# A hybrid attention and convolution layer: attention steps three to a dense unit, key loads moved ahead, attention rows reloaded in pairs

## The chip, the cores and the metric

The kernel runs on one core of one Trainium2 chip. The metric is the device time of one execution in microseconds. A run with the hardware profiler gives the trace that the rows below come from.

## The reference

One layer for 512 latent and 128 context tokens of width 2048, in float32: a modulated norm; one input projection into a gated convolution branch, grouped queries, keys, values and two branch gates; the two branches; a gated sum, an output projection, and a routed expert network. Cut to what the change touches:

```python
h = rmsnorm(x, n1g) * (1 + sc1) + sh1
glu_in, q, k, v, ga, gb = jnp.split(h @ w_in, SPLITS, axis=-1)
conv_out = conformer_conv(glu_in, ...)
# per head, 16 heads in 4 key groups of 4 query heads; blocks of 128 queries;
# latent blocks read keys of a window of +-128 tokens and all 256 cached context keys,
# the context block reads the 128 context keys
m = jnp.maximum(jnp.max(sc, axis=-1, keepdims=True), sk)
p = jnp.exp(sc - m)
den = jnp.sum(p, axis=-1, keepdims=True) + jnp.exp(sk - m)
att = einsum(p / den, vals)
attn_out = att @ w_attn_out
mixed = (sigmoid(ga) * conv_out + sigmoid(gb) * attn_out) @ w_out
```

The modulation vectors (adaLN) come from `silu(cond) @ w_ada`, 96 blocks of 128 columns.

## The kernel before, in words

Every matrix product in float32 is made of three products of split operands: the weights of a unit (128 output columns, 2048 x 128) are loaded into `raw`, a ring of four slots; ScalarE casts them into `whi` (L846), VectorE subtracts to get `wlo` (L1185), and TensorE runs 96 matmuls (L579 to L581), six for each of the sixteen k-steps, against `hhi` and `hlo`, the split activations. The split of a unit is made two units ahead. An adaLN block is 1 MB of weights too, goes through the same ring, and is used unsplit (L563), closed by a small transpose (L566) that frees its slot; ScalarE reads its result out (L859, L853).

The program of each engine is written out by hand; engines wait for each other by semaphores, each engine working in its own order. The stage of interest makes the 32 units of the branch gates (tanh, L1007, stored to `gates_tanh`, L455). It is a loop over the four key groups, eight units to a pass. Beside the dense work of the pass run:

- the 20 attention steps of the group (4 heads x 5 query blocks, `STEPS`; the fifth block of each head, j = 4, is the short context one). A step on TensorE: scores (L653 to L656), a part of the unit's dense k-steps, transposes of the normalised probabilities (L666), an adaLN block if it is the unit's first or second step, and the product with the values (L678). On VectorE: maxima (L1304, L1308, L1315), then sums and normalisation (L1324 to L1329). On ScalarE: exponentials (L960 to L968), the copy of the transposed probabilities (L975, L977), the copy of the head's output (L984), which POOL's queue stores into `att` (L451);
- 16 adaLN blocks, two to a unit;
- 62 taps of the depthwise convolution on VectorE (L1344, L1348).

`CUT` deals the steps to units: before, 2 and 3 alternately, so the eighth unit of a group has three. The weights' splits for later units (`next_unit`) stand, on ScalarE and VectorE, behind the first step's softmax of the following unit, except that of the eighth unit, which stands at the end of the pass, ahead of the next pass's first step. In the order of the ring the loads of a unit are its own weights, then the two adaLN blocks; each waits until the load four places earlier has been used up.

POOL's queue loads a group's keys (`ktg`), values (`vg`) and first queries (`qh`) at the top of the pass, behind all stores of the pass before. Behind the last group it waits for the stores of outputs and gates, then reloads the attention rows, one 128 x 640 block to a load, into a ring of four (`att4`, L469); ScalarE casts each into `hhi` (L1028), VectorE subtracts into `hlo` (L1381), and the first unit of the attention projection takes each k-step as it comes.

```python
cuts = [KT * x // len(steps) for x in range(len(steps) + 1)]
for x, n in enumerate(steps):
    qk(i, n)
    dense(d, d, k % 2, k % 2, hhi, hlo, cuts[x], cuts[x + 1], 0, KT)
    turn(i, n)
    if x < 2:
        ada_unit(...)
    pv(i, n)
```

Of the kernel before, what the change touches and what calls it, by code (L numbers as in the profile page):

```python
# [41 lines left out]
US = 8  # L42
# [26 lines left out]
def build(nc, a, out):  # L69
# [62 lines left out]
    zt, o = at("zt", [128, CT, ZW], F32, Y0)  # L132
    ctmp, o = at("ctmp", [128, CO], F32, o)
    ktg, o = at("ktg", [128, N + PAST], F32, o)
    vg, o = at("vg", [128, (N + PAST) // 128, HD], F32, o)
# [24 lines left out]
    gl, o = at("gl", [128, 2, N], F32, o)  # L160
    att4, _ = at("att4", [128, 4, N], F32, o - 2 * N * 4)
    mo, o = at("mo", [128, 2, N], F32, o)
# [90 lines left out]
    vec_done = sem("vec_done")  # L253
    act_done = sem("act_done")
    gsc_ready = sem("gsc_ready")
# [50 lines left out]
    NS = len(STEPS)  # L306
    CUT = [NS * k // US for k in range(US + 1)]

# [65 lines left out]
    def pool_program(pool):  # L374
# [65 lines left out]

        with pool.Fori(0, NKV) as i:
            load_group(i)
            load_q(i, 1)
            for k in range(US):
                for n in range(CUT[k], CUT[k + 1]):
                    h, j = STEPS[n]
                    if j == 0 and 0 < h and h + 1 < GROUP:
                        load_q(i, h + 1)
                    pool.wait_ge(att_out, i * NS + (n + 1) + 1)
                    settle()  # L450
                    pool.dma_start(at_d[i * GROUP + h][:, 128 * j:128 * j + 128],  # L451
                                   ao[:, n % 2, :]).then_inc(att_stored[n % 2], 16)
                pool.wait_ge(th_ready, i * US + (k + 1))
                settle()
                pool.dma_start(th_d[i * US + k], th[:, k % 2, :]).then_inc(th_stored[k % 2], 16)  # L455


        for b in range(2):
            pool.wait_ge(att_stored[b], 16 * (NKV * NS // 2))
            pool.wait_ge(th_stored[b], 16 * (SN // 2))  # L460

# [3 lines left out]

        for m in range(KT):
            if m >= 4:
                pool.wait_ge(attn_lo, m - 3)
            pool.dma_start(att4[:, m % 4, :], at_d[m]).then_inc(attn_loaded[m % 4], 16)  # L469
        pool.wait_ge(attn_lo, KT)  # L470
# [83 lines left out]
    def tensor_program(pe):  # L554
# [127 lines left out]
        with pe.Fori(0, SN // US) as i:  # L682
            for k in range(US):
                d = i * US + (QN + GN + k)
                dense_start(d, QN + GN + k, i, US)
                steps = list(range(CUT[k], CUT[k + 1]))
                cuts = [KT * x // len(steps) for x in range(len(steps) + 1)]
                for x, n in enumerate(steps):
                    qk(i, n)
                    dense(d, d, k % 2, k % 2, hhi, hlo, cuts[x], cuts[x + 1], 0, KT)  # L690
                    turn(i, n)
                    if x < 2:
                        at_ = G_S + 3 * k + 1 + x
                        ada_unit(at_ % RAW, at_ // RAW + i * (3 * US // RAW),
                                 i * (2 * US) + (RAW + A1 + 2 * k + x), pt[:, 1, :], row1[0:2, :])
                    pv(i, n)
        pe.wait_ge(ada_read, RAW + ADA)
# [143 lines left out]
    def scalar_program(act):  # L841
# [144 lines left out]
        def stage_s(i):  # L986
# [5 lines left out]
            for k in range(US):  # L992
                steps = list(range(CUT[k], CUT[k + 1]))
                for x, n in enumerate(steps):
                    softmax(i, n)
                    if x == 0 and k:
                        next_unit(k - 1)
                    turned(i, n)
                    if x < 2:
                        at_ = G_S + 3 * k + 1 + x  # L1000
                        ada_read_out(at_ % RAW, at_ // RAW + i * (3 * US // RAW), i * (2 * US) + (A1 + 2 * k + x - 1),
                                     pt[:, 1, :], row1[0:2, :])
                    head_out(i, n)
                act.wait_ge(dense_mm, i * US + (QN + GN + k + 1 + CREDIT))
# [21 lines left out]
        for m in range(KT):  # L1026
            act.wait_ge(attn_loaded[m % 4], 16 * (m // 4 + 1))
            nc.scalar.copy(hhi[:, m, :], att4[:, m % 4, :]).then_inc(attn_hi, 1)  # L1028

# [143 lines left out]
    def vector_program(vec):  # L1173
# [180 lines left out]
        def stage_s(i):  # L1354
            def next_unit(k):
                slot, use, d2 = ahead(i, k, US, G_S, 3, QN + GN, SN, G_T)
                split_lo(slot, use, d2, k % 2)

            for k in range(US):
                steps = list(range(CUT[k], CUT[k + 1]))  # L1360
                for x, n in enumerate(steps):
                    maxima(i, n)
                    normalise(i, n)
                    if x == 0 and k:
                        next_unit(k - 1)
                    conv(i, k, x, len(steps))
            next_unit(US - 1)
# [11 lines left out]
        for m in range(KT):  # L1379
            vec.wait_ge(attn_hi, m + 1)  # L1380
            nc.vector.tensor_tensor(hlo[:, m, :], att4[:, m % 4, :], hhi[:, m, :].bitcast(F32),  # L1381
                                    ALU.subtract).then_inc(attn_lo, 1)
# [440 lines left out]
```

## Time and profile before

| | |
|---|---|
| median of 3 runs | 3484.56 us (3480.05 to 3485.72) |
| the profiled execution | 3483.9 us |
| its span, first to last instruction | 3482.3 us, mean granted clock 0.975 |
| TensorE busy | 3293.6 us, 95% |
| VectorE busy | 1938.5 us, 56% |
| ScalarE busy | 1391.7 us, 40% |
| DMA | 746 MB, mean 214 GB/s |

The span is shorter than the profiled execution's own time by what lies around it. The stage with the attention steps stands from about 744 to 1661 us of the span, the first unit of the attention projection behind it to 1696. Busy time of TensorE is of pipelined matmuls whose ends are modelled; the granted clock is given as a share of full speed.

### The profile page before, as it was taken

The page shows a single profiled execution, that of the slowest core. Times are in us where ns is not written, and L with a number is a line of the kernel's source. Part 1 is how long each engine was busy: PE and PEld are TensorE (multiplying, and loading weights), DVE is VectorE, ACT ScalarE, POOL GpSimd, SP SyncE. Part 2 cuts the span into 40 slices and gives each one's busy share as a digit, 9 for nine tenths or more (in the row PEclk, how much of TensorE's full clock was granted, in tenths as well). Part 3 has the DMA queues.
Part 4 walks back from the last instruction along what each step waited for, and adds up shares of the span by engine and source line. Part 5 has one row for each costly group of instructions (what it writes and reads, how often), then busy time and mean ns, then how long its engine had stood idle before and what let it go on. Part 6 is the DMA issues. An engine that isn't in the chain of part 4 may idle for free.

```text
span 3482.3 us, 52715 instructions
## 1 busy us (share of the span) xinstructions
PE 3293.6 (95%) x20485; PEld 2765.2 (79%) x20485; DVE 1938.5 (56%) x1987; ACT 1391.7 (40%) x1669; POOL 280.5 (8%) x445
## 2 busy tenths in 40 slices
PE   7699999999989899899899999959999999999995
PEld 5499999998888888788799999946666666666663
DVE  3223332135444445454642533369998999899994
ACT  2311111122323232223331212137777777777774
POOL 0001110000010000000100111110000000000000
PEclk9899999999999999999999999979999999999997
DMA  7533332223333333333433454379999999999994
GB/s 295 202 109 127 124 117 99 81 81 139 134 136 143 133 143 131 134 141 130 168 119 118 179 163 136 99 259 364 400 376 374 391 390 371 381 391 386 374 386 146
DMA packets 124020, 745.97 MB, mean 214 GB/s; under 512 B 16720, under 2 KB 27024, under 8 KB 44096
## 3 DMA queue, kind: packets, MB, share of 16 engines
q1 hardware_dynamic: 96368, 631.28, 47.5%
q0 software_dynamic: 27504, 112.60, 10.5%
q8 instruction: 107, 1.75, 0.2%
q14 instruction: 41, 0.34, 0.0%
HBM read 681.60 MB, written 55.66 MB: 212 GB/s over the span
## 4 chain that ended last, share of the span: by engine, by line
PE 79%; DVE 7%; issue 5%; ACT 2%; DMA 2%; POOLq 0%; SPq 0%; POOL 0%; ACTq 0%; DVEq 0%
PE pu L813 20%; PE pu L579 15%; PE pu L580 15%; PE pu L581 15%; PE pt L563 7%; DVE elo L1603 4%; PE pt L678 2%; ACT ehi L1108 2%; PE ps L653 1%; DVE xe L1615 1%; PE pt L666 1%; PE ps L654 1%; DMA tokens_acc<-ysl,idx_all 1%; PE ps L784 1%; DMA att<-att 1%
## 5 line engine op out<-in xcount | busy, mean ns | idle before, releaser
L579 PE MATMUL pu<-hhi,whi 128*128 128x320 f32 x3328 | 1050.3, 316 | 50.1 <-DVE wlo L1185 32.1
L580 PE MATMUL pu<-hlo,whi 128*128 128x320 f32 x3328 | 1033.4, 311 | 0.0
L581 PE MATMUL pu<-hhi,wlo 128*128 128x320 f32 x3328 | 1033.2, 310 | 0.0
L1603 DVE TENSOR_TENSOR elo<-ering,ehi 128x2048 fp32r<-128x2048 f32 x384 | 874.7, 2288 | 107.0 <-ACT ehi L1108 103.8
L1108 ACT CAST ehi<-ering 128x2048 fp32r<-128x2048 f32 x384 | 731.3, 1912 | 238.3 <-PE pu L813 238.2
L579 PEld LDWEIGHTS pu<-hhi,whi 128*128 128x128 f32 x3328 | 629.9, 189 | 54.1 <-issue 43.1
L580 PEld LDWEIGHTS pu<-hlo,whi 128*128 128x128 f32 x3328 | 629.9, 189 | 2.0
L581 PEld LDWEIGHTS pu<-hhi,wlo 128*128 128x128 f32 x3328 | 629.4, 189 | 0.0
L846 ACT CAST whi<-raw 128x2048 fp32r<-128x2048 f32 x112 | 213.0, 1902 | 481.7 <-PE pu L581 463.5
L1185 DVE TENSOR_TENSOR wlo<-raw,whi 128x2048 fp32r<-128x2048 f32 x112 | 256.6, 2291 | 255.4 <-ACT whi L846 255.0
L813 PE MATMUL pu<-ehi,xhi 128*80 128x512 f32 x1024 | 322.0, 395 | 2.2
L813 PE MATMUL pu<-ehi,xlo 128*80 128x512 f32 x1024 | 320.3, 394 | 0.0
L813 PE MATMUL pu<-elo,xhi 128*80 128x512 f32 x1024 | 320.0, 393 | 0.0
L563 PE MATMUL pt<-raw,cond 128*2 128x128 f32 x2048 | 233.9, 273 | 0.0
L1348 DVE SCALAR_TENSOR_TENSOR ctmp<-zt,taps,ctmp 128x670 f32<-128x670 f32 x232 | 212.5, 916 | 29.2 <-DVE ctmp L1348 19.8
L813 PEld LDWEIGHTS pu<-ehi,xhi 128*80 128x80 f32 x1024 | 149.4, 148 | 89.8 <-DVE elo L1603 9.3
L813 PEld LDWEIGHTS pu<-elo,xhi 128*80 128x80 f32 x1024 | 151.6, 148 | 85.5 <-issue 0.7
L813 PEld LDWEIGHTS pu<-ehi,xlo 128*80 128x80 f32 x1024 | 151.5, 148 | 85.6 <-issue 0.7
L563 PEld LDWEIGHTS pt<-raw,cond 128*2 128x2 f32 x2048 | 168.7, 85 | 57.2 <-issue 10.7
L813 PE MATMUL pu<-ehi,hthi 128*80 128x512 f32 x512 | 162.9, 399 | 0.0
L813 PE MATMUL pu<-elo,hthi 128*80 128x512 f32 x512 | 159.8, 393 | 0.0
L813 PE MATMUL pu<-ehi,htlo 128*80 128x512 f32 x512 | 159.7, 393 | 0.0
(264 smaller groups left out, 2854.9 us busy)
## 6 DMA issues: line engine op xcount, KB each, us to landing
ering<-in_w_experts SPq DMA_DIRECT2D x384, 1024.0 KB, 8.2
raw<-in_w_ada SPq DMA_DIRECT2D x96, 1024.0 KB, 5.0
raw<-in_w_in SPq DMA_DIRECT2D x72, 1024.0 KB, 4.9
raw<-in_w_attn_out SPq DMA_DIRECT2D x16, 1024.0 KB, 5.2
raw<-in_w_out SPq DMA_DIRECT2D x16, 1024.0 KB, 4.9
gates_tanh<-th POOLq DMA_DIRECT2D x32, 320.0 KB, 3.2
gl<-gates_tanh POOLq DMA_DIRECT2D x32, 320.0 KB, 3.4
raw<-in_w_conv_out SPq DMA_DIRECT2D x8, 1024.0 KB, 4.8
```

The costliest lines, as they stand in the source:

```text
L563: last = nc.tensor.matmul(bank[0:2, 0:128], cond[:, kt, :], raw[:, slot, kt * 128:kt * 128 + 128], start=kt == 0, stop=kt == KT - 1)
L579: nc.tensor.matmul(o, whi[:, dk, w:w + 128], hi[:, kt, cols], start=kt == 0, stop=False)
L580: nc.tensor.matmul(o, whi[:, dk, w:w + 128], lo[:, kt, cols], start=False, stop=False)
L581: last = nc.tensor.matmul(o, wlo[:, dk, w:w + 128], hi[:, kt, cols], start=False, stop=kt == kts - 1)
L653: nc.tensor.matmul(ps[:, 0, 0:128 * (hi - lo)], qb, ktg[:, 128 * lo:128 * hi], start=True, stop=True)
L678: last = nc.tensor.matmul(pt[:, 0, 0:128], vg[:, v, :], pt_sb[:, 128 * b:128 * b + 128], start=b == 0, stop=b == len(vs) - 1)
L813: last = nc.tensor.matmul(pu[0:SLOTS, 2 * (h % 2) + c, :], left, ring[:, j % AHEAD, w:w + 512], start=k == 0 and left is hi and ring is eh ...
L846: nc.scalar.copy(whi[:, dk, :], raw[:, slot, :]).then_inc(hi_ready, 1)
L1108: nc.scalar.copy(ehi[:, j % AHEAD, :], ering[:, slot, :]).then_inc(ex_hi, 1)
L1185: nc.vector.tensor_tensor(wlo[:, dk, :], raw[:, slot, :], whi[:, dk, :].bitcast(F32), ALU.subtract).then_inc(lo_ready, 1)
L1348: nc.vector.scalar_tensor_tensor(out=dst, in0=ztf[:, ds(zb, CO)], scalar=w, in1=ctmp[:, :], op0=ALU.mult, op1=ALU.add).then_inc(conv_done, 1)
L1603: nc.vector.tensor_tensor(elo[:, j % AHEAD, :], ering[:, slot, :], ehi[:, j % AHEAD, :].bitcast(F32), ALU.subtract).then_inc(ex_lo, 1)
```

## The change

`CUT` becomes three steps to a unit: units one to six of a group have three steps, the seventh two, the eighth none. The eighth unit's dense work is still made in two parts, each with its adaLN block behind it; VectorE makes all its taps in one piece. The loads of the next group's keys, values and queries move from the top of the pass to before the store of the eighth unit's gates; the loop on POOL's queue runs over three groups, the first group's loads stand ahead of it and the last group behind it. The attention rows come back in pairs, eight loads of 640 KB, into a ring of eight blocks (`att8`) that lies over the keys, values and attention buffers; the wait for the gates' stores moves behind these loads. An unused semaphore goes.

```diff
@@ memory
+    att8, _ = at("att8", [128, 8, N], F32, o)
     ktg, o = at("ktg", [128, N + PAST], F32, o)
...
-    att4, _ = at("att4", [128, 4, N], F32, o - 2 * N * 4)
@@ steps of a unit
-    CUT = [NS * k // US for k in range(US + 1)]
+    CUT = [min(3 * k, NS) for k in range(US + 1)]
@@ POOL's queue
-        with pool.Fori(0, NKV) as i:
-            load_group(i)
-            load_q(i, 1)
+        def stage_s(i, following):
             for k in range(US):
                 for n in range(CUT[k], CUT[k + 1]):
...
+                if k == US - 1 and following is not None:
+                    load_group(following)
+                    load_q(following, 1)
                 pool.wait_ge(th_ready, i * US + (k + 1))
...
+        load_group(0)
+        load_q(0, 1)
+        with pool.Fori(0, NKV - 1) as i:
+            stage_s(i, i + 1)
+        stage_s(NKV - 1, None)
 
         for b in range(2):
             pool.wait_ge(att_stored[b], 16 * (NKV * NS // 2))
-            pool.wait_ge(th_stored[b], 16 * (SN // 2))
...
-        for m in range(KT):
+        for m in range(KT // 2):
             if m >= 4:
-                pool.wait_ge(attn_lo, m - 3)
-            pool.dma_start(att4[:, m % 4, :], at_d[m]).then_inc(attn_loaded[m % 4], 16)
+                pool.wait_ge(attn_lo, 2 * (m - 3))
+            pool.dma_start(att8[:, 2 * (m % 4):2 * (m % 4) + 2, :],
+                           at_d[2 * m:2 * m + 2].rearrange("h p n -> p h n")).then_inc(attn_loaded[m % 4], 16)
+        for b in range(2):
+            pool.wait_ge(th_stored[b], 16 * (SN // 2))
@@ TensorE, the units
                 steps = list(range(CUT[k], CUT[k + 1]))
-                cuts = [KT * x // len(steps) for x in range(len(steps) + 1)]
-                for x, n in enumerate(steps):
-                    qk(i, n)
-                    dense(d, d, k % 2, k % 2, hhi, hlo, cuts[x], cuts[x + 1], 0, KT)
-                    turn(i, n)
+                parts = max(2, len(steps))
+                for x in range(parts):
+                    n = steps[x] if steps else None
+                    if steps:
+                        qk(i, n)
+                    dense(d, d, k % 2, k % 2, hhi, hlo, KT * x // parts, KT * (x + 1) // parts, 0, KT)
+                    if steps:
+                        turn(i, n)
                     if x < 2:
...
-                    pv(i, n)
+                    if steps:
+                        pv(i, n)
@@ ScalarE, the same; then the attention rows
-            act.wait_ge(attn_loaded[m % 4], 16 * (m // 4 + 1))
-            nc.scalar.copy(hhi[:, m, :], att4[:, m % 4, :]).then_inc(attn_hi, 1)
+            act.wait_ge(attn_loaded[m // 2 % 4], 16 * (m // 8 + 1))
+            nc.scalar.copy(hhi[:, m, :], att8[:, m % 8, :]).then_inc(attn_hi, 1)
@@ VectorE, the units
-                for x, n in enumerate(steps):
-                    maxima(i, n)
-                    normalise(i, n)
+                parts = max(1, len(steps))
+                for x in range(parts):
+                    if steps:
+                        maxima(i, steps[x])
+                        normalise(i, steps[x])
                     if x == 0 and k:
                         next_unit(k - 1)
-                    conv(i, k, x, len(steps))
+                    conv(i, k, x, parts)
```

TensorE at the end of a group's pass. The second adaLN block of the eighth unit (`raw`, `cond`, 16 matmuls, waits for its slot's load) and what follows it stood so before:

```order
L563 MATMUL pt<-raw,cond 2x128 [waits ada_read]
L563 MATMUL pt<-raw,cond 2x128 x15
L566 MATMUL pt<-ident,row_73 128x2
L676 REGISTER_ALU
L678 MATMUL pt<-pt_sb,vg 128x128 [waits att_pt]
L678 MATMUL pt<-pt_sb,vg 128x128 x3
L656 MATMUL ps<-ktg,qh 128x128 [waits att_pt,att_exp]
```

and stands so now (the branch leads to the scores of the next group's first step):

```order
L569 REGISTER_ALU [waits raw_loaded3]
L571 MATMUL pt<-raw,cond 2x128 [waits ada_read]
L571 MATMUL pt<-raw,cond 2x128 x15
L574 MATMUL pt<-ident,row_73 128x2
L690 REGISTER_ALU
L690 COMPARE_AND_BRANCH
```

Before, a whole step with a third of the unit's dense work followed the block; now the pass ends with it.

ScalarE at the same place, from the second adaLN read-out to the pass's end and the next pass's first exponential. Before:

```order
L859 COPY row_73<-pt 2x128 [waits raw_freed3]
L853 ISA
L853 ACTIVATE mod<-pt,bada 128x2
L983 ISA [waits att_pv]
L984 COPY ao<-pt 128x128 [waits att_stored0]
L966 ACTIVATE pexp,dn<-ps,nm 128x128 [waits att_nm]
...
L1007 ACTIVATE th<-pu 128x640 [waits th_stored1,dense_mm]
L1010 REGISTER_ALU
L846 CAST whi<-raw 128x2048 [waits th_ready,dense_mm,raw_loaded3]
L1014 ISA [waits hi_ready]
```

Now:

```order
L871 COPY row_73<-pt 2x128 [waits raw_freed3]
L865 ISA
L865 ACTIVATE mod<-pt,bada 128x2
L1020 REGISTER_ALU
L1023 ACTIVATE th<-pu 128x640 [waits th_stored1,dense_mm]
L1026 REGISTER_ALU
L858 CAST whi<-raw 128x2048 [waits th_ready,dense_mm,raw_loaded3]
L1030 ISA [waits hi_ready]
L1031 ISA [waits att_stored0]
L1033 REGISTER_ALU [waits th_stored1,att_stored1,th_stored0]
L1033 COMPARE_AND_BRANCH
L972 ACTIVATE pexp,dn<-sm,nm 128x256 [waits att_nm]
```

The cast of weights from slot 3, the slot that the second adaLN block frees (`raw_freed3`), was parted from that block by a whole step and is now parted from it by the read-out and the tanh.

## Rows read from the trace of the kernel before

**Rows 1.** The page, part 1: busy time, share of the span, instructions of each engine.
```profile
PE 3293.6 (95%) x20485; PEld 2765.2 (79%) x20485; DVE 1938.5 (56%) x1987; ACT 1391.7 (40%) x1669; POOL 280.5 (8%) x445
```
**Rows 2.** Waits of TensorE: waiting group, releaser: us in total, times, longest.
```profile
PE ps L653 <- DMA ktg<-in_cache_k: 25.9, 3, 8.9
...
PE pu L579 <- DVE hlo L1381: 14.3, 6, 9.8
...
PE pt L678 <- ACT pt_sb L975: 5.7, 16, 0.4
...
PE pt L666 <- DVE pn L1329: 0.6, 1, 0.6
```
**Rows 3.** The chain in order of time, first group's end: start us, us, what.
```profile
965.98 0.27 ACT ao L984
...
970.46 3.75 DMA ktg<-in_cache_k
```
**Rows 4.** Stretches: us, busy (count) of PE, PEld, DVE, ACT, POOL, PEclk, DMA share, GB/s.
```profile
974.50:979.40 4.90, 4.85 (x16) 4.53 (x17) 1.13 (x4) 1.24 (x5) 0.00 (x0) 0.50 0.21 82
1700.00:1710.00 10.00, 10.00 (x70) 10.00 (x69) 9.86 (x2) 0.00 (x0) 0.00 (x0) 1.00 0.41 139
```
**Rows 5.** Timeline, first group's end: start us, us, engine, line, op [idle before <-releaser].
```profile
958.18 0.22 PE L566 MATMUL pt<-ident,row 2*128 2x2 f32 x1
...
958.44 0.26 ACT L859 COPY row<-pt 2x128 f32<-2x128 f32 x1 [3.15 <-PE pt L566]
...
958.58 0.33 SPq L321 DMA_DIRECT2D raw<-in_w_in  x1
...
967.01 1.90 ACT L846 CAST whi<-raw 128x2048 fp32r<-128x2048 f32 x1 [0.17 <-ACT th L1007]
```
**Rows 6.** Weight load L321, from issue: the one of 958.6, then of 1168.5.
```profile
DMA to landing us min/median/max: 4.9/4.9/4.9
...
DMA to landing us min/median/max: 7.3/7.3/7.3
```
**Rows 7.** Timeline where the stage begins.
```profile
744.42 0.59 PE L653 MATMUL ps<-ktg,qh 128*128 128x256 f32 x2
...
744.68 1.90 ACT L846 CAST whi<-raw 128x2048 fp32r<-128x2048 f32 x1 [11.36 <-PE pu L581]
...
753.12 0.66 PE L666 MATMUL pt<-ident,pn 128*128 128x128 f32 x4 [0.64 <-DVE pn L1329]
```
**Rows 8.** Timeline: a step with five key blocks, and a short third step.
```profile
877.31 0.27 PE L666 MATMUL ps<-ident,pn 128*128 128x128 f32 x1
...
877.62 0.58 ACT L975 COPY pt_sb<-pt 128x512 f32<-128x512 f32 x1 [4.72 <-PE ps L666]
878.10 0.27 ACT L977 COPY pt_sb<-ps 128x128 f32<-128x128 f32 x1
...
1660.99 0.49 PE L678 MATMUL pt<-pt_sb,vg 128*128 128x128 f32 x2 [0.35 <-ACT pt_sb L975]
```
**Rows 9.** Timeline, first unit of the attention projection.
```profile
1671.45 0.60 PE L579 MATMUL pu<-hhi,whi 128*128 128x320 f32 x1 [9.82 <-DVE hlo L1381]
...
1696.26 1.90 ACT L846 CAST whi<-raw 128x2048 fp32r<-128x2048 f32 x1 [3.76 <-PE pu L581]
```
**Rows 10.** The chain in order of time, behind the last group.
```profile
1663.28 2.44 DMA gates_tanh<-th
...
1666.87 6.12 DMA att<-att
...
1673.01 0.73 ACT hhi L1028
...
1673.77 0.83 DVE hlo L1381
```
**Rows 11.** DMA issues: KB, median us to landing; then L321 at 1654 to 1655.
```profile
att<-att POOLq DMA_DIRECT2D x16, 320.0 KB, 3.6
...
DMA to landing us min/median/max: 5.1/6.4/7.8
```

More of the change, by code:

```diff
@@ L253, in build @@
     vec_done = sem("vec_done")
-    act_done = sem("act_done")
     gsc_ready = sem("gsc_ready")
@@ L993, in stage_s @@
                 steps = list(range(CUT[k], CUT[k + 1]))
-                for x, n in enumerate(steps):
-                    softmax(i, n)
+                for x in range(max(2, len(steps))):
+                    n = steps[x] if steps else None
+                    if steps:
+                        softmax(i, n)
                     if x == 0 and k:
                         next_unit(k - 1)
-                    turned(i, n)
+                    if steps:
+                        turned(i, n)
                     if x < 2:
@@ L1002, in stage_s @@
                                      pt[:, 1, :], row1[0:2, :])
-                    head_out(i, n)
+                    if steps:
+                        head_out(i, n)
                 act.wait_ge(dense_mm, i * US + (QN + GN + k + 1 + CREDIT))
@@ L1360, in stage_s @@
                 steps = list(range(CUT[k], CUT[k + 1]))
-                for x, n in enumerate(steps):
-                    maxima(i, n)
-                    normalise(i, n)
+                parts = max(1, len(steps))
+                for x in range(parts):
+                    if steps:
+                        maxima(i, steps[x])
+                        normalise(i, steps[x])
                     if x == 0 and k:
                         next_unit(k - 1)
-                    conv(i, k, x, len(steps))
+                    conv(i, k, x, parts)
             next_unit(US - 1)
@@ L1380, in vector_program @@
             vec.wait_ge(attn_hi, m + 1)
-            nc.vector.tensor_tensor(hlo[:, m, :], att4[:, m % 4, :], hhi[:, m, :].bitcast(F32),
+            nc.vector.tensor_tensor(hlo[:, m, :], att8[:, m % 8, :], hhi[:, m, :].bitcast(F32),
                                     ALU.subtract).then_inc(attn_lo, 1)
```

## The prediction

> **What bounds the kernel now.** I read the page's totals first: TensorE is busy 95% of the span [rows 1], so what TensorE does, or is kept from doing, is the time, and work of the other engines costs nothing unless TensorE ends up waiting for it. Next, TensorE's own waits, longest first: in the stage that the change touches (about 744 to 1696 us) two entries matter, 25.9 us in three waits of the score matmuls L653 for the keys, and 14.3 us in six waits for the split attention rows (`hlo`, L1381), the longest 9.8 us [rows 2]. The chain around the first group's end says why the keys are late: ScalarE copies the last head's output at 965.98, and only behind that, and behind two stores and a query load on the POOL queue, is the key load issued; it ends at 974.21 [rows 3]. The stretches add a second price: behind the idle time come 4.9 us at a granted clock of 0.50 (the 1.2 GHz level), against 1.00 later [rows 4]. So each group's end costs about 8.6 us of idle and 2.4 us of half speed, 11 us, three times over.
>
> All sums below are against the profiled execution, 3483.9 us; the median of the runs shown is 0.7 us higher, 3484.6.
>
> **1. Key wait removed.** The next group's loads are now issued before the store of the eighth unit, when the last attention step is one whole unit past. Cover: that unit, at least 13.7 us of dense work (96 matmuls at 70 in 10.00 us [rows 4]). Gain 25.9 us of idle, and 3 x 2.4 = 7.3 us of half speed.
>
> **2. What is late next.** ScalarE and VectorE split the weights of a group's tenth dense unit (the next group's second) at the end of the group's code, ahead of the first softmax and the first maxima of the next group. Those weights go into the ring slot that the eighth unit's second adaLN block frees. Before, that slot was freed with a whole attention step still to come: TensorE's closing transpose of the adaLN block starts at 958.18, SP issues the load at 958.58, and the cast starts at 967.01 right behind the tanh, with no wait for the load [rows 5]. After, the eighth unit is two halves of dense work with an adaLN block behind each, so this block is the last thing in the unit. Call the start of its transpose f. The load is issued at f+0.4 and lands 4.9 us later [rows 6], at f+5.3; ScalarE casts, VectorE subtracts, and only then come maxima, exponential and normalisation of step 0. The same sequence stands once in the trace, where the stage begins: from the start of the cast at 744.68 to the transposes at 753.12 it takes 8.44 us [rows 7]. So the first transposes of the new group can run at f+13.75.
>
> TensorE is there earlier. At the stage's beginning the scores start at 744.42 and TensorE, with eight of the sixteen k-steps under the step, is at the transposes 0.64 us before they may run [rows 7]: 8.06 us. Now a first part holds five k-steps: 18 matmuls fewer, at 70 in 10.00 us [rows 4] 2.6 us less, so 5.5 us. Scores start about 0.2 after f: ready at f+5.7. Wait 13.75 - 5.7 = 8.05, three times 24.2 us. An idle stretch like the old one should again bring the lower clock; I take the same 7.3 us. **Group ends: -25.9 - 7.3 + 24.2 + 7.3 = -1.7 us.** The load is the unknown: the same kind of load one unit earlier took 7.3 us [rows 6], which adds 2.4 per group end; the clock may cost 0 or, as after the wait at 1671, some 3.9 us each.
>
> **3. Third steps without cover.** A unit has two adaLN blocks. Behind the transposes of a step's first and second part such a block runs while ScalarE copies the probabilities; a third step has none, and TensorE waits for the copy. Before, the four third steps of a group were all the short context step (one transpose, wait 0.35 us, 5.7 in 16) [rows 2, 8]. After, the steps stand three to a unit, so the third ones are steps 2, 5, 8, 11, 14 and 17: three with five key blocks, two with four, one short. With five blocks the last transpose ends at 877.31 + 0.27 = 877.58, the first copy runs from 877.62 for 0.58 and the second ends at 878.37; with 0.05 us from copy to matmul (my estimate of the signalling) the wait is 0.84. With four blocks there is the first copy alone: 0.04 + 0.58 + 0.05 = 0.67 [rows 8]. Per group 3 x 0.84 + 2 x 0.67 + 0.35 - 4 x 0.35 = 2.8 us, **four groups +11.2 us**. Ends: 0 if something fills the wait (I see nothing in TensorE's order that could), 11.2 as worked.
>
> **4. First step of the stage.** Its transposes may not run before 753.12 whatever TensorE does, and it arrives 2.6 us earlier: **+2.6 us**.
>
> **5. Steps with five k-steps over them** (the other long first and second parts): the wait for the normalised rows L1329 occurred once among 80 steps [rows 2], and the thirds that are now long have six k-steps. Hidden, 0.
>
> **6. Behind the last group.** Before: the last unit ends at about 1661.4, its gates' store has to land (2.44 us in the chain) before the first attention load is issued, half a microsecond ahead of 1666.87, and TensorE restarts at 1671.45; the first unit of the projection lasts until ScalarE's cast of 1696.26 can start [rows 9, 10]. That is 24.8 us for 96 matmuls which, at 70 in 10.00 us, need 13.7: the ring of four lets a load go only when a row is split, and one such load took 6.12 us in the chain [rows 10]. After: the store is no longer waited for, -2.4, but tanh stands behind the adaLN read-out, two small copies of which one is 0.26 [rows 5], so about 0.5, so the first load goes out about 3.0 after the unit's end. It is 640 KB now. Bounds: a single 320 KB row block took 3.6 median; 1 MB loads issued together took 5.1 and 7.8 [rows 11]. I take 5.2, since two weight loads are in flight beside it, then cast 0.73, subtraction 0.83 [rows 10] and 0.2 of signalling: restart 10.0 after the unit's end, as before. Then all four pairs are under way and the fifth is issued after two rows are split, about 8 k-steps ahead of need, so TensorE runs through: 13.7 plus 3.2 for a half-speed stretch (between 2.4 and 3.9) = 16.9. **Gain 7.9 us.** Ends: 2 if the pairs land as late as 7.8, 11 if there is no half speed at all.
>
> By the Trainium skill (DMA: Bandwidth & Descriptors, Anatomy of one DMA — SWDGE (gpsimd) path) such a transfer takes 2.0 us and bytes over 436 GB/s, so 3.5 us for a pair; the sum would be 1.7 us lower by it. The trace's 3.6 us median for half the bytes speaks against relying on it here.
>
> **Sum**: -1.7 + 11.2 + 2.6 - 7.9 = +4.2; 3483.9 + 4.2 = 3488.1, and 3489 beside the median. A measurement here can tell about 0.2% from no change, 7 us: from 3477.6 to 3491.5 is the same. So: no difference that can be measured, leaning to slower.
>
> **Rivals.**
> - *The group ends are simply freed.* Needs the tenth unit's weights to be in place when tanh ends. For: they were, before [rows 5]. Against: the slot is freed by the unit's last act. Time: 3489 - 24.2 - 7.3 = 3457. Chance 0.12.
> - *The weight load at the group end lands late* (slower). Place: the load issued at f+0.4, with an adaLN block's load right behind it and the gates' store beside it. Price: 7.3 instead of 4.9, +2.4 us at each of three ends, 3496. It decides from about 0.8 us of lateness per end, where the sum passes 3491.5. For: the load one unit earlier took 7.3. Against: this very load took 4.9 at its old place [rows 6]. Chance 0.23.
> - *The third steps cost nothing* because TensorE's waits there are taken up by others I don't see: 3489 - 11.2 = 3478. Chance 0.10.
>
> The forecast has the remaining 0.55.
>
> **The numbers.** Range 3475 to 3501: down to the cheap-thirds case with 3 us to spare for part 6, up to late loads together with a part 6 that gives only 3; the freed case is left out. Faster: the freed case and a few per cent of the cheap-thirds one, 0.15. Slower by over 7 us: most of the late-load case and a third of the forecast's own, which lies only 2.5 us under the bound, 0.39. Same: 0.46.
>
> **What would show it.** TensorE's waits: none left for the keys; three of about 8 us of the transposes for the normalised rows at the group ends, and in ScalarE's row of that cast a wait for the weight load. Waits for the probability copy: 24 instead of 16, and about 17 us instead of 5.7. First projection unit: about 17 us, one or two short gaps. Granted clock: still three half-speed stretches at the group ends. I am wrong at the root if the transposes at a group's start don't wait, or if the half-speed stretches are gone.

## The result, and the profile after

Six runs of each kernel.

| | before | after |
|---|---|---|
| median, us | 3484.37 | 3498.91 |
| lowest to highest, us | 3480.05 to 3485.72 | 3495.91 to 3501.42 |
| ratio, with 95% interval | | 1.0043 (1.003 to 1.0056) |
| profiled execution, its span, us | 3483.9, 3482.3 | 3501.42, 3499.8 |

The change makes the kernel 14.5 us slower, twice what I said a measurement here can tell. The forecast was 3489, "no difference that can be measured, leaning to slower". The time lies inside the range, but the likeliest case was 10 us too fast, and by the bound of 7 us set there the result is the "slower" case, which had 0.39, and not "same", which had 0.46. The profiled execution of after is the slowest of its six; its trace shows 14.5 us up to the first unit of the output projection, and the 3 us more that its span has lie behind that.

TensorE is still the engine that sets the time: the page's totals, to be held against [rows 1].

```profile
PE 3296.5 (94%) x20485; PEld 2765.6 (79%) x20485; DVE 1938.3 (55%) x1987; ACT 1390.9 (40%) x1669; POOL 277.6 (8%) x437
```

TensorE's waits, which answer to [rows 2] (waiting group, releaser: us in total, times, longest):

```profile
PE pt L674 <- DVE pn L1345: 21.8, 4, 7.5
...
PE pu L587 <- DVE hlo L1399: 14.1, 1, 14.1
...
PE pt L686 <- ACT pt_sb L989: 10.1, 12, 0.8
...
PE ps L661 <- issue: 7.0, 3, 2.5
...
PE pt L686 <- ACT pt_sb L987: 6.8, 12, 0.7
```

The key wait (25.9 us) is gone, as meant. In its place stand the transposes' wait for the normalised rows `pn` (21.8 in 4), the waits for the probability copy (16.9 in 24, before 5.7 in 16), and one that I had not named: 7.0 us in three "issue" waits ahead of the scores, where TensorE waits for nothing that the profile shows.

Where the time went is best read from one instruction that both kernels have: ScalarE's tanh on a group's eighth unit, which starts when that unit is done. Starts from the timelines; the last column is the cast behind the projection's first unit ([rows 9]; 1710.77 after).

| us | group 1 | group 2 | group 3 | group 4 | first projection unit |
|---|---|---|---|---|---|
| before | 966.14 | 1197.96 | 1429.61 | 1661.68 | 1696.26 |
| after | 972.95 | 1209.37 | 1445.26 | 1679.25 | 1710.77 |
| difference | 6.8 | 11.4 | 15.7 | 17.6 | 14.5 |
| added in this stretch | +6.8 | +4.6 | +4.2 | +1.9 | -3.1 |

The first group's end, timeline (start us, us, engine, line, op [idle before <-releaser]), to be read against [rows 5, 7]:

```profile
972.38 0.22 PE L574 MATMUL pt<-ident,row 2*128 2x2 f32 x1
...
972.77 0.33 SPq L320 DMA_DIRECT2D raw<-in_w_in  x1
...
974.41 0.54 POOL L455 DMA_DIRECT2D gates_tanh<-th  x1 [17.01 <-ACT th L1023]
975.07 0.67 PE L661 MATMUL ps<-ktg,qh 128*128 128x256 f32 x2 [2.48 <-issue]
977.90 1.90 ACT L858 CAST whi<-raw 128x2048 fp32r<-128x2048 f32 x1 [4.27 <-DMA raw<-in_w_in]
979.83 2.29 DVE L1201 TENSOR_TENSOR wlo<-raw,whi 128x2048 fp32r<-128x2048 f32 x1 [12.27 <-ACT whi L858]
982.50 1.28 ACT L972 ACT_TABLE_LOAD   x1 [2.71 <-DMA gates_tanh<-th]
985.53 0.43 DVE L1320 TENSOR_REDUCE mx<-ps 128x1 f32<-128x256 f32 x1 [3.41 <-issue]
...
989.36 1.12 PE L674 MATMUL pt<-ident,pn 128*128 128x128 f32 x4 [7.25 <-DVE pn L1345]
```

The chain is the one of the forecast: the closing transpose of the adaLN block (f = 972.38), the weight load at once, the split behind it, the softmax behind that. Its cast is at f+5.5 (forecast f+5.3). But between VectorE's subtraction, which ends at 982.12, and the maxima at 985.53 lie 3.41 us in which VectorE waits for nothing either, and the transposes come at f+17.0 instead of f+13.75. Both "issue" gaps lie where an engine's loop over the groups goes back to its start.

The granted clock around it (stretch: us, busy (count) of PE, PEld, DVE, ACT, POOL, then PEclk, DMA share, GB/s), with the stage's beginning ahead, to be held against [rows 4]:

```profile
754.10:757.50 3.40, 3.40 (x18) 2.06 (x16) 0.50 (x1) 0.14 (x1) 0.00 (x0) 0.50 0.00 0
975.96:979.40 3.44, 3.44 (x14) 3.35 (x14) 0.00 (x0) 1.50 (x1) 0.00 (x0) 0.51 0.98 363
...
986.20:989.30 3.10, 0.00 (x0) 0.00 (x0) 1.47 (x7) 1.24 (x5) 0.00 (x0) 0.50 0.00 0
989.40:993.00 3.60, 3.60 (x17) 2.24 (x18) 1.37 (x2) 0.58 (x1) 0.00 (x0) 0.50 0.02 5
```

There are now two half-speed stretches per group end (behind the gap at the loop's turn, and behind the wait for `pn`), with 7.0 us of work in them at this end, against 4.9 before (6.3 against 5.5 and 8.9 against 5.4 at the next two); and one at the stage's beginning, 3.4 us, that the kernel before did not have.

Behind the last group, timeline, to be read against [rows 9, 10]:

```profile
1679.07 5.81 SPq L320 DMA_DIRECT2D raw<-in_w_attn_out  x3
...
1680.52 0.54 POOL L455 DMA_DIRECT2D gates_tanh<-th  x1 [21.07 <-ACT th L1023]
1681.09 2.85 POOL L474 DMA_DIRECT2D att<-att  x4
1688.39 0.26 ACT L865 ACTIVATE mod<-pt,bada 128x2 f32<-128x2 f32 x1 [6.40 <-DMA gates_tanh<-th]
1691.89 1.35 ACT L1044 CAST hhi<-att 128x640 fp32r<-128x640 f32 x2 [3.24 <-DMA att<-att]
...
1693.70 0.61 PE L587 MATMUL pu<-hhi,whi 128*128 128x320 f32 x1 [14.09 <-DVE hlo L1399]
```

and, from issue to landing, of the gates' store of 1680.52 and of the four pairs of 1681.09:

```profile
DMA to landing us min/median/max: 7.7/7.7/7.7
...
DMA to landing us min/median/max: 10.7/12.4/13.8
```

The first pair goes out 1.8 us after the unit's end, sooner than I had worked out. But of the three 1 MB weight loads that the first row gathers, two go out 2.0 and 1.1 us ahead of it (1679.07 and 1679.94) and the third 3.4 us behind it (1684.54), and it lands in 10.7 us where I took 5.2.

### The profile page after: what moved, and what is told of

Its sections match the earlier page's. It is cut to its first block, busy times and chain, and to the rows that moved or that the text cites. A ratio compares the mean times of both kernels' runs of the same rounds, so it can differ in the third digit from the quotient of the medians.

```text
span 3499.8 us, 52614 instructions
## 1 busy us (share of the span) xinstructions
PE 3296.5 (94%) x20485; PEld 2765.6 (79%) x20485; DVE 1938.3 (55%) x1987; ACT 1390.9 (40%) x1669; POOL 277.6 (8%) x437
## 4 chain that ended last, share of the span: by engine, by line
PE 78%; DVE 7%; issue 5%; ACT 3%; DMA 2%; POOL 0%; SPq 0%; DVEq 0%; ACTq 0%; POOLq 0%
PE pu L825 20%; PE pu L587 15%; PE pu L588 15%; PE pu L589 15%; PE pt L571 7%; DVE elo L1621 3%; PE pt L686 2%; ACT ehi L1124 2%; DVE xe L1633 1%; PE ps L661 1%; PE pt L674 1%; PE ps L662 1%; DMA att<-att 1%; DMA tokens_acc<-ysl,idx_all 1%; PE ps L796 1%
## 5 line engine op out<-in xcount | busy, mean ns | idle before, releaser
L1364 DVE SCALAR_TENSOR_TENSOR ctmp<-zt,taps,ctmp 128x670 f32<-128x670 f32 x232 | 212.6, 916 | 29.8 <-DVE ctmp L1364 20.4
```

The lines of the kernel that those rows point to most:

```text
L1364: nc.vector.scalar_tensor_tensor(out=dst, in0=ztf[:, ds(zb, CO)], scalar=w, in1=ctmp[:, :], op0=ALU.mult, op1=ALU.add).then_inc(conv_done, 1)
```

## The experiments

Eleven kernels, in three lots. The kernel before was timed beside each lot: 3484.10 in the first (26 runs), 3483.38 in the second (21), 3484.28 in the third (9).

### The third steps: one k-step held back

In the changed kernel (and below, in the kernel before), the last of a unit's sixteen k-steps is put behind the third step's transposes:

```diff
-                    dense(..., KT * x // parts, KT * (x + 1) // parts, 0, KT)
+                    held = 1 if x == 2 else 0
+                    dense(..., KT * x // parts, KT * (x + 1) // parts - held, 0, KT)
                     if steps:
                         turn(i, n)
+                    if held:
+                        dense(..., KT - 1, KT, 0, KT)
```

On the changed kernel: 

> The change with the last of the sixteen k-steps of a three-step unit held back: on TensorE it runs between the third step's transposes and its product with the values, 0.86 us of work over a wait of 0.35 to 0.84. Theory A (third steps wait uncovered for the copy of the probabilities): the waits for that copy, 16.9 us in 24, fall below 2 us and the time to 3482 (3480 to 3485). Rival: the waits are taken up by others behind them, so that filling them only moves them; time 3495 or more.

Measured 3478.50 (3477.78 to 3480.92, ten runs), ratio to before 0.9985 (0.9975 to 0.9995): 20.4 us under the changed kernel. The waits for `pt_sb` are gone from TensorE's list, the others stay (23.0 for `pn`, 6.5 "issue"). Theory A holds, and a third step costs 20.4 / 24 = 0.85 us.

On the kernel before: 

> The kernel before with one sixteenth of the unit held back behind the third step's transposes, in the units with three steps (four of eight). Theory A (a third step costs 0.7 to 0.8 us because nothing lies between its transposes and its last product; the kernel before has the same loss in half its units): the waits for pt_sb go, 5.7 us in 16, and the time falls by 5 to 6 us, to 3478.5 (3477 to 3481), where the changed kernel with the same edit is (3478.5). Rival (the waits are replaced by others, since a third step's chain is late anyway): 3482 to 3485.

Measured 3470.65 (3469.39 to 3472.08), ratio 0.9964 (0.9951 to 0.9978): 12.7 us gained where the waits add up to 5.7 and I expected 5 to 6. So a third step costs 0.79 us there too, though the list of waits shows 0.35. The timeline of TensorE tells why. The kernel before, a short third step:

```profile
799.08 0.31 PE L581 MATMUL pu<-hhi,wlo 128*128 128x320 f32 x1
799.22 0.27 PE L666 MATMUL pt<-ident,pn 128*128 128x128 f32 x1
799.85 0.49 PE L678 MATMUL pt<-pt_sb,vg 128*128 128x128 f32 x2 [0.35 <-ACT pt_sb L975]
800.39 0.67 PE L653 MATMUL ps<-ktg,qh 128*128 128x256 f32 x2
```

and the same step with the k-step held back:

```profile
798.08 0.27 PE L666 MATMUL pt<-ident,pn 128*128 128x128 f32 x1
798.11 0.39 PE L579 MATMUL pu<-hhi,whi 128*128 128x320 f32 x1
...
799.08 0.38 PE L678 MATMUL pt<-pt_sb,vg 128*128 128x128 f32 x2
799.30 0.60 PE L653 MATMUL ps<-ktg,qh 128*128 128x256 f32 x2
```

Starts are what counts in a pipelined engine. With the gap it is 0.63 us from the transpose's start to the product's and 0.54 from there to the next scores; without it the next matmul starts 0.03 behind the transpose, and the scores 0.22 behind the product. That is 0.60 + 0.32 = 0.92 us. The six matmuls in between take 0.97 us from start to start there, 0.11 more than six take at 70 in 10.00 us, so about 0.81 us are saved, for a wait that the list gives as 0.35. The net price of the change's regrouping is therefore 20.4 - 12.7 = 7.7 us by the medians, not the 11.2 of the forecast. It isn't sharp: up to the fourth group's eighth tanh the profiled executions gained 18.6 and 13.6 us, 4.9 apart.

### The loops' turn: the passes written out

```diff
-        with pe.Fori(0, SN // US) as i:
+        for i in range(SN // US):
```

and in the same way on ScalarE and VectorE.

> The change with the four passes of the gate stage written out one after the other on TensorE, ScalarE and VectorE, no loop. Theory (the turn of the loop costs TensorE 2.0 to 2.5 us ahead of the scores and VectorE 3.3 us ahead of the maxima): both idle times go, the transposes at the first two group ends come 3 us earlier as at the third, nothing is won at the third; 3498.9 - 6 = 3493 (3490 to 3495), the waits for the normalised rows grow to some 6 us each since TensorE arrives earlier. Rival (these idle times are the engines' instruction loads slowed by the 2 MB of weights in flight, loop or no loop): they stay and the time with them, 3499.

Measured 3490.73 (3488.92 to 3493.32), 8.2 us under the changed kernel, ratio 1.002 (1.001 to 1.0029). The "issue" wait is gone from TensorE's list, and on VectorE the maxima follow the subtraction directly, where [3.41 <-issue] stood:

```profile
977.21 2.29 DVE L1201 TENSOR_TENSOR wlo<-raw,whi 128x2048 fp32r<-128x2048 f32 x1 [12.95 <-ACT whi L858]
979.66 0.42 DVE L1320 TENSOR_REDUCE mx<-ps 128x1 f32<-128x256 f32 x1 [0.15 <-DVE wlo L1201]
...
983.61 1.12 PE L674 MATMUL pt<-ident,pn 128*128 128x128 f32 x4 [7.95 <-DVE pn L1345]
```

From ScalarE's read-out behind the adaLN block (972.63 after, 970.24 here) to the transposes it was 16.7 us and is 13.4: the forecast's length of the chain, once the turn is out of it. The three waits at the group ends are now 7.95, 7.79 and 7.55 us; the forecast had 8.05. So the gaps are the loops' turn. TensorE's own, in front of the scores, is off the path as long as the transposes wait: its part moved into the wait for `pn`, 26.2 us in 4 instead of 21.8.

### The split in front of the softmax, and a wait behind it

The split of the next group's second unit, on ScalarE and VectorE, is moved behind the first step's exponential (and normalisation):

```diff
                     if x == 0 and k:
                         next_unit(k - 1)
+                    if x == 0 and k == 0:
+                        split_hi(*raw_use(G_S, 3, US, i, 1), i * US + (QN + GN + 1), 1)
...
-            next_unit(US - 1)
+            if isinstance(i, int):
+                next_unit(US - 1)
```

> The change with one thing moved: the split of a group's second unit (ScalarE's cast, VectorE's subtraction) stands behind the first step's softmax and normalisation of its own pass instead of at the end of the pass before. Theory A (the split ahead of the first step makes the new wait): TensorE's waits of the transposes for the normalised rows, 21.8 us in four, fall below 2 us, the 2.0 to 2.5 us ahead of the scores at three group ends stay, half-speed stretches at the group ends shrink or go; 3498.9 - 20 - up to 10 = 3466 to 3479. Rival B (the loop's turn on the engines, which VectorE's 3.3 us of idle at the first two ends shows, makes it): at least two waits of 3 us or more remain and the time stays above 3485.

Measured 3487.64 (3483.47 to 3492.39, ten runs), ratio 1.0009 (1.0 to 1.0019). 11.3 us gained: less than theory A asks for, and the time stays above 3485 as rival B has it, but only one wait of 3 us or more remains, not two. The waits for `pn` fell to 9.6 us in 3 (2.5, 4.4 and 2.7, at the group ends). Part of the gain is not of the group ends: the split of the stage's first pass moved too, its wait of 3.28 us and the half speed behind it are gone, and the first group's eighth tanh comes 4.3 us sooner (968.63). What remains is a third thing:

```profile
970.10 0.54 POOL L455 DMA_DIRECT2D gates_tanh<-th  x1 [17.01 <-ACT th L1027]
...
974.17 0.21 DVE L1338 TENSOR_SCALAR nm<-mx,negsink 128x1 f32<-128x1 f32 x1 [0.16 <-DVE mx L1331]
978.07 1.28 ACT L974 ACT_TABLE_LOAD   x1 [8.75 <-DMA gates_tanh<-th]
979.36 0.51 ACT L974 ACTIVATE pexp<-sm,nm 128x256 f32<-128x256 f32 x1
...
981.66 0.66 PE L674 MATMUL pt<-ident,pn 128*128 128x128 f32 x4 [2.48 <-DVE pn L1352]
```

The row bias `nm` is ready at 974.38, but ScalarE ends each group with a wait for the gates' store, and that store, issued behind the weight loads, takes 7.5 us to land. A load of ScalarE's function table (1.28 us) comes behind it, and the exponential starts 5 us late. So this wait was moved too, to the tanh that writes over the buffer, with ScalarE's passes written out:

```diff
-                if k >= 2:
+                if i * (US // 2) + k // 2 > 0:
                     act.wait_ge(th_stored[k % 2], (i * (US // 2) + k // 2) * 16)
...
-                act.wait_ge(th_stored[b], (i * (US // 2) + US // 2) * 16)
```

> The split moved behind the first step's softmax, as in the first experiment, and now ScalarE's wait for the gates' store moved too, from the end of a pass to the tanh that writes over the buffer (ScalarE's four passes written out). Theory C (that wait is what held the first softmax, 979.36 where its maximum was ready at 974.17): the transposes' waits at the three group ends go from 9.6 us to under 3, and with the half-speed stretches behind them the time falls by 7 to 12 us from 3487.6, to 3478 (3475 to 3481). Rival (VectorE's own loop turn and the key products' wait end last anyway): waits stay over 7 us, time 3485 to 3489.

Measured 3469.22 (3467.14 to 3471.49), ratio 0.996 (0.9946 to 0.9973): 18.4 us less again, more than the 7 to 12 expected. No wait for `pn` is left in TensorE's list. The first group's end now:

```profile
974.88 0.21 DVE L1337 TENSOR_SCALAR nm<-mx,negsink 128x1 f32<-128x1 f32 x1 [0.16 <-DVE mx L1330]
975.22 0.51 ACT L974 ACTIVATE pexp<-sm,nm 128x256 f32<-128x256 f32 x1 [4.81 <-DVE nm L1337]
...
978.42 0.60 PE L674 MATMUL pt<-ident,pn 128*128 128x128 f32 x4
```

With the 9.6 us of waits for `pn` and 0.6 of the "issue" waits went most of the half speed behind them: 6.7 us of work at half speed are left in the stage, where the kernel with only the split moved had 18.9, so 6.1 us. Together that is 16.3 us, and the two profiled executions differ by 16.1; the 2 us up to the medians' 18.4 I can't place. ScalarE's written-out passes are in it: the table load of 1.28 us, which stood at the first two ends, is gone with its loop, so not all of the gain is the store's wait.

### The slot freed earlier

A rival cure, on the changed kernel: both adaLN blocks of the eighth unit in its first half (behind k-steps 4 and 8), so that its ring slot comes free 7 us sooner.

> The changed kernel with both modulation blocks of the eighth unit in its first half, so that the last slot comes free about 7 us ahead of the unit's end. Theory A (the split waits for its load, issued at the unit's end and 5.1 us under way): ScalarE's split starts at the unit's end, about 5 us sooner, the three long transposes' waits fall from 7.3, 7.5 and 3.8 us to 1 to 3 each, and with shorter stretches at half speed the kernel gains 12 to 20 us: 3483 (3479 to 3487). Rival (the two split copies in front of the first softmax and VectorE's loop turn are what the transposes wait for, the load being hidden by them): under 5 us gained, 3494 to 3499.

Measured 3479.95 (3475.94 to 3483.29, eleven runs), ratio 0.9988 (0.9979 to 0.9997): 19.0 us under the changed kernel, as theory A has it. The weight load goes out at 965.65 and the cast stands right behind the tanh; the waits for `pn` fall to 7.6 us in 3, of which 3.3 is the stage's first step; the idle time ahead of the scores stays, 8.5 us in 3:

```profile
973.62 1.90 ACT L861 CAST whi<-raw 128x2048 fp32r<-128x2048 f32 x1 [0.17 <-ACT th L1026]
```

The late slot is therefore what made the group ends long. It can be cured at either end, by an earlier load or by not letting the softmax stand behind it.

### Behind the last group

The pairs alone, on the kernel before (its steps and key loads as they were, and the rows loaded in pairs into a ring of eight, issued ahead of the wait for the gates' store):

```diff
-        for m in range(KT):
-            if m >= 4:
-                pool.wait_ge(attn_lo, m - 3)
-            pool.dma_start(att4[:, m % 4, :], at_d[m]).then_inc(attn_loaded[m % 4], 16)
+        for m in range(KT // 2):
+            if m >= 4:
+                pool.wait_ge(attn_lo, 2 * (m - 3))
+            pool.dma_start(att8[:, 2 * (m % 4):2 * (m % 4) + 2, :], ...).then_inc(attn_loaded[m % 4], 16)
```

> The kernel before with the pairs into a ring of eight alone, the steps and the key loads as they were. Theory A (the sum of the parts as the trace of after shows them: from the last unit's end to the first unit of the stage after it 31.8 us instead of 34.8, the first pair landing late behind three weight loads): 3.0 us faster than before, 3481 (3478.5 to 3484). Rival (my step on record, the first pair landing in 5.2 us): 7.9 us faster, 3476.5. Rival (the pairs gain nothing by themselves, and the 3 us come from the dense unit without steps in front of them): 3484 to 3486.

Measured 3479.47 (3476.5 to 3482.7, eleven runs), ratio 0.9989 (0.998 to 0.9998): 3.9 us faster by the medians, nearest to theory A. Its profiled execution, the second fastest of the eleven, does better: last tanh at 1660.73, cast at 1688.56, 27.8 us against 34.6 before and 31.5 in the changed kernel. Here the first pair, issued at 1663.98, is cast at 1668.65, 4.7 us later, close to the 5.2 of the forecast. What the pairs can give depends on what is on the queues when they start.

The weight loads held back, on the changed kernel (SyncE's fourth load of the projection and all behind it wait until eight rows are split):

```diff
+                    if k == 3:
+                        sp.wait_ge(attn_lo, 8)
```

> The change with SP's fourth weight load of the attention projection, and all behind it, held until eight attention rows are split. Theory A (the pairs and the gates' store land late because 2 MB of weights were issued 2 us ahead of them): the store lands in under 3.5 us instead of 7.7, the first pair in under 6 us instead of 10.7, TensorE's wait of 14.1 us for the first rows falls to 7 to 9 us, time 3492 to 3494. Rival (loads of 640 KB from POOL's queue are slow by themselves): first pair over 8 us, time within 2 us of 3499. For neither does the held weight load come late: its split is due some 30 us later.

Measured 3498.02 (3497.57 to 3500.33), ratio 1.0042 (1.0028 to 1.0056): no gain. The first step happened. The gates' store and the first pair now land, from issue, in

```profile
DMA to landing us min/median/max: 2.5/2.5/2.5
...
DMA to landing us min/median/max: 4.6/4.6/4.6
```

against 7.7 and 10.7, so it was the weight loads that held both up, and TensorE's longest wait fell from 14.1 to 8.0 us. But the loads, let go together at 1692.12 to 1693.34, fell on the later pairs (the last takes 10.1 us); the casts of the last rows wait again, and the unit's cast comes at 1707.92, with 9.7 us of work at half speed against 5.9:

```profile
1684.56 1.35 ACT L1049 CAST hhi<-att 128x640 fp32r<-128x640 f32 x2 [2.36 <-DMA att<-att]
...
1702.54 1.35 ACT L1049 CAST hhi<-att 128x640 fp32r<-128x640 f32 x2 [3.50 <-DMA att<-att]
1707.92 1.90 ACT L863 CAST whi<-raw 128x2048 fp32r<-128x2048 f32 x1 [4.03 <-PE pu L594]
```

### All cures together

The changed kernel with the split and the store's wait moved, the k-step held back and the passes of the three engines written out.

> The changed kernel with the four cures that the runs so far bear out, together: the split behind the first softmax, the wait for the gates' store at its tanh, a sixteenth held back in the third steps, and the passes of TensorE, ScalarE and VectorE written out. If the costs add (Theory A): from 3469.2 the third steps give 18 to 20 us and the turn of TensorE's loop 6 to 8 us: 3443 (3440 to 3448). Rival (with the waits gone the softmax chain is late again somewhere, in steps that now stand closer together): waits for pn come back, 3450 to 3465.

Measured 3437.05 (3435.42 to 3437.71, four runs), ratio 0.9864 (0.9849 to 0.9879): 47.2 us, 1.4%, faster than the kernel before, 6 us better than the costs added up to. A group now takes 217.98 us from eighth tanh to eighth tanh, the same three times over, where it took 231.8 before and 236.4 in the first of the changed kernel, and no half-speed stretch is left in the stage. The one wait over 1 us that is left in the stage and at its end:

```profile
PE pu L587 <- DVE hlo L1411: 13.1, 1, 13.1
```

The same, and the weight loads held until fourteen rows are split:

> The same with SyncE's fourth weight load of the output projection, and those behind it, held until attn_lo stands at 14, when all pairs are in. Theory A (the weight loads ahead of and beside the pairs are what makes these land in 10 to 14 us; held until 8 they only delayed the later pairs): TensorE's restart comes 5 to 6 us sooner and nothing delays the later pairs, 4 to 8 us faster than without it, 3438 (3435 to 3441). Rival (three weight loads already on their way when the pairs start are enough to delay them, or the held loads now come late for the units): within 2 us of the version without it.

Measured 3437.21 (3436.48 to 3437.94, four runs): no difference. The first unit's cast comes 4.4 us sooner (1642.82 against 1647.22), and TensorE then waits as much longer for the statistics of the layer norm in the projection:

```profile
PE ps L607 <- DVE ls L1441: 5.4, 1, 5.4
```

against 0.9 without the hold. The timelines show why. Those statistics stand on VectorE behind the first product with the gates (`mo`), which waits for the gates to be loaded back. Without the hold:

```profile
1645.33 1.11 POOL L468 DMA_DIRECT2D gl<-gates_tanh  x2 [7.48 <-DVE hlo L1411]
...
1648.65 0.82 DVE L1485 SCALAR_TENSOR_TENSOR mo<-gl,pu 128x640 f32<-128x640 f32 x1 [3.66 <-DMA gl<-gates_tanh]
```

and with it:

```profile
1641.90 1.10 POOL L473 DMA_DIRECT2D gl<-gates_tanh  x2 [9.15 <-DVE hlo L1416]
...
1649.14 0.82 DVE L1490 SCALAR_TENSOR_TENSOR mo<-gl,pu 128x640 f32<-128x640 f32 x1 [7.58 <-DMA gl<-gates_tanh]
```

The gates' load goes out 3.4 us sooner and its product starts 0.5 later: the load takes 7.1 us instead of 3.2, behind the three weight loads let go at 1639.50 to 1640.72. So the hold has moved the collision once more, onto the gates. Whether a hold that spares them too gives the 4.4 us was not tried.

The kernel before, with its own placement of the steps, the k-step held back and the pairs:

> The kernel before with its own steps and key loads, a sixteenth held back in its third steps, and the pairs. If the two add: 3470.65 less 3.9, 3466.8 (3465 to 3469). It is what the step placement of before gives with the same cures; the difference to the version with all cures is what the changed placement is worth once its new waits are gone (Theory A: over 15 us; rival, the placement gives nothing: under 5 us).

Measured 3468.94 (3464.59 to 3472.23), ratio 0.9953 (0.9939 to 0.9966). The changed kernel with all cures is 31.9 us faster than this. What it is faster by can be read: this kernel still has the key wait, 26.6 us in 3, and 14.8 us of work at half speed behind it, which costs 7.4 us more: 34.0 us together. The cured one has neither. So the change was worth having for the key loads moved ahead, and what hid that were its new waits; that three steps to a unit give anything by themselves no run shows. The split, the store's wait and the written-out passes were not tried on the kernel before.

## Why the prediction was right or wrong

- **Part 1, key wait gone:** right. No key wait is left.
- **Part 2, what is late next:** the mechanism was right in each link and is borne out by two cures. The load landed in 5.1 us (4.9 taken), the cast came at f+5.5 (5.3). The step that failed is "only then come maxima": I took the sequence from [rows 7], where no loop turns between subtraction and maxima, and 3.3 to 3.4 us of VectorE's turn were missing at two ends (at the third, followed by the last pass, which is straight-line code, it is 0.3). In the same way "scores start about 0.2 after f" left out TensorE's turn, 2.0 to 2.5 us at each end. The two largely cancel in the idle time, 18.6 us for `pn` and 7.0 "issue", 25.6 against 24.2; that this sum comes out is luck. But they are two gaps in place of one, and the half speed behind them costs 11.1 us (22.2 us of work) instead of the 7.3 that I carried over; before, it was 8.0 (15.9 us of work), the first end being the cheapest. By these rows the group ends stand at 25.6 + 11.1 - 25.9 - 8.0, before rounding +2.9, not -1.7.
- **Part 3, third steps:** the waits are as worked out, 16.9 us against 16.8. The price was mis-sized, on both sides: 0.85 us per step after and 0.79 before, whatever the list says, so 7.7 instead of 11.2.
- **Part 4, first step of the stage:** its wait is 3.28, as 0.64 + 2.6 has it. Missing was that this wait brings a half-speed stretch of 3.4 us, 1.7 lost: 4.3 instead of 2.6. The kernel with the split moved, which has neither, is 4.3 us ahead at the first group's eighth tanh.
- **Part 5:** right. The `pn` list has four waits, three at the group ends and that of the stage's first step.
- **Part 6, behind the last group:** the first unit took 17.1 us from restart to cast, against 16.9. The failed term is the landing of the first pair: 10.7 us where I took 5.2 and named 7.8 as the other end. Two weight loads are in flight beside it, as the forecast says, but they go out at the last unit's end, 2.0 and 1.1 us ahead of it, and with them held it landed in 4.6. Gain 3.1 instead of 7.9. The estimate of 3.5 us for such a pair by the Trainium skill (DMA: Bandwidth & Descriptors, Anatomy of one DMA — SWDGE (gpsimd) path) is under everything measured here: the shortest of the changed kernel's eight pairs took 4.5 us, the longest 13.8.

| us | forecast | measured |
|---|---|---|
| group ends | -1.7 | +2.9 |
| third steps | +11.2 | +7.7 (by the two runs with the k-step held back) |
| first step | +2.6 | +4.3 |
| behind the last group | -7.9 | -3.1 |
| not placed | | +2.7 |
| sum | +4.2 | +14.5 |

The 2.7 is what the 14.5 us leave. Held against the stretches of the table of tanh starts it is 0.5 to 0.9 us in each of the four groups, the first too, which has no group end ahead of it. So it belongs to every pass and not to the group ends; the third steps, whose price is known to a few us only, may be it, but no run shows that.

Of the rivals, "the group ends are freed" fell: every group end has its new wait. "The weight load lands late" gave about the right time, 3496, for a wrong reason: its load was on time. What landed late was the gates' store, 7.6 us at the first end, which didn't yet decide there, and the pairs. What gave the time were the longer half speed, the third steps and the late pairs. "The third steps cost nothing" fell.

## What to carry to other kernels

When a wait is removed, follow every instruction that comes after it in program order on each engine, up to and over the loop's end: here a weight split, a wait for a store and the loop's own turn stood unseen under the key wait, and together they cost more than it did. Price a gap in TensorE's stream from start to start of its matmuls, with the half speed behind it, not by the idle time in the list of waits. And when transfers are issued right at a stage's end, look at which queue gets there first; holding the others back moved the collision in both trials, onto the later pairs and onto the gates, and won nothing.

## What the runs showed of the hardware

- An engine's way back to the start of a long loop body costs time that no semaphore explains: 2.0 to 2.5 us on TensorE, 3.3 to 3.4 on VectorE; with the passes written out both are gone. By the Trainium skill (Runtime: NRT & Kernel Launch, Instruction fetch mechanics) a taken branch to code outside the two pages that are held has to fetch it before going on. The runs agree with that in sign; the page gives no duration, and that fetching is the cause wasn't tested by itself.
- ScalarE's loop brought a load of its function table, 1.28 us, ahead of the first exponential behind the first two group ends (the kernel before, the changed kernel, the one with the split moved); with its passes written out none stands there.
- A wait of 0.35 us in TensorE's list cost about 0.8 us of starts.
- A store of 320 KB on the POOL queue landed in 2.4 us by the median of 32, and in 7.6 to 7.8 with two 1 MB weight loads issued up to 1.6 us ahead; behind the last group it took 7.7, and 2.5 with the weight loads held. A 640 KB load landed there in 10.7 us with two 1 MB loads issued 2.0 and 1.1 us ahead, and in 4.6 with them held; in the kernel before with the pairs, where none went out just ahead, it took 4.6 too.
- The granted clock fell to 0.50 (the 1.2 GHz level) for 3.4 us behind an idle stretch of 3.28 us at the stage's beginning, and likewise behind one of 2.48 at the first group's end; each stretch costs 1.7 us.
